# A fused decoder layer with 32 experts: second-layer weights in column halves, the last expert scattered and normed by halves, the last three experts loaded in 2 MB transfers

## The reference

```
logits = rms_norm(x, g_ffn) @ w_router + b_router       # 256 x 32
top_v, top_i = top_k(logits, 4);  gates = softmax(top_v)
for each expert e, for the tokens that chose it:
    u     = xb @ w_e1[e] + b_e1[e]                      # 1024 -> 2048
    x_glu = min(u[..., ::2], 7);  x_lin = clip(u[..., 1::2], -7, 7)
    act   = x_glu * sigmoid(1.702 * x_glu) * (x_lin + 1)
    y     = act @ w_e2[e] + b_e2[e]                     # 1024 -> 1024
x   = x + sum over a token's experts of gate * y
out = rms_norm(x, g_final)
```

## Time and profile before

| what | value |
|---|---|
| median of the runs | 1183.01 us |
| the profiled execution | 1181.18 us |
| its span | 1179.2 us |
| TensorE matmuls busy | 1131.8 us, 96% |
| TensorE weight loads busy | 548.3 us, 47% |
| VectorE busy | 430.9 us, 37% |
| ScalarE busy | 256.7 us, 22% |
| moved by DMA | 447.66 MB, mean 380 GB/s |
| the chain that ended last | TensorE 64%, DMA 30%, VectorE 4%, ScalarE 1% |

### The profile page before, as it was taken

The page is one execution under the profiler, slowest core; times in us unless marked ns, Lnnn a source line. Parts: engine busy times, 40 slices in busy tenths (PEclk is TensorE's granted clock), DMA queues, the critical chain, the costliest instruction groups (busy, mean ns, idle before and its releaser), DMA issues.

```text
span 1179.2 us, 17758 instructions
## 1 busy us (share of the span) xinstructions
PE 1131.8 (96%) x7323; PEld 548.3 (47%) x7323; DVE 430.9 (37%) x836; ACT 256.7 (22%) x441; POOL 21.4 (2%) x22
## 2 busy tenths in 40 slices
PE   7999999999999999999999999999999999999997
PEld 6988999984333333333333333333333333333332
DVE  6889855964222222222222222222222222222223
ACT  5466746332111111111111111111111111111112
POOL 1000200011000000000000000000000000000000
PEclk9999999999999999999999999999999999999999
DMA  7645336789999999999999999999999999999995
GB/s 297 241 147 211 130 140 241 297 336 422 429 426 428 434 430 429 435 430 430 435 431 431 428 437 430 431 428 438 430 429 436 431 430 428 439 428 430 430 425 227
DMA packets 26225, 447.66 MB, mean 380 GB/s; under 512 B 3072, under 2 KB 3456, under 8 KB 5680
## 3 DMA queue, kind: packets, MB, share of 16 engines
q1 hardware_dynamic: 25760, 446.76, 90.0%
q10 hardware_dynamic: 432, 0.42, 0.1%
HBM read 446.12 MB, written 1.05 MB: 379 GB/s over the span
## 4 chain that ended last, share of the span: by engine, by line
PE 64%; DMA 30%; DVE 4%; ACT 1%; issue 1%; DVEq 0%; another core or an unknown queue 0%; SPq 0%; ACTq 0%
PE PS L907 35%; DMA ring<-wexp 29%; PE PS L628 15%; PE PS L900 3%; PE PS L892 3%; PE PS L923 1%; PE PS L677 1%; PE PS L753 1%; DVE ROW L1777 1%; DVE ROW L1780 1%; DVE BRW L1773 1%; PE PS L727 1%; DMA ring<-wblk 1%; DVE ROW L1774 0%; PE PS L990 0%
## 5 line engine op out<-in xcount | busy, mean ns | idle before, releaser
L907 PE MATMUL PS<-ring,MX 128*64 128x512 f32 x1536 | 349.9, 597 | 17.5 <-DMA ring<-wexp 16.3
L907 PEld LDWEIGHTS PS<-ring,MX 128*64 128x64 f32 x1536 | 103.1, 136 | 229.7 <-issue 195.7
L1262 ACT ACTIVATE TAB<-BRW 128x256 f32<-128x256 f32 x64 | 26.7, 417 | 593.6 <-DVE BRW L1773 593.6
L907 PE MATMUL PS<-ring,TAB 128*64 128x512 f32 x512 | 120.0, 600 | 3.5 <-DMA ring<-wexp 3.5
L907 PE MATMUL PS<-EXT,TAB 128*64 128x512 f32 x512 | 119.8, 600 | 3.2 <-DMA EXT<-wexp 3.2
L907 PE MATMUL PS<-EXT,MX 128*64 128x512 f32 x512 | 116.9, 598 | 0.9
L1773 DVE TENSOR_SCALAR BRW<-PS 128x256 f32<-128x256 f32 x64 | 27.2, 425 | 241.1 <-PE PS L907 241.1
L628 PE MATMUL PS<-slot_R 128*128 128x256 f32 (+2 forms) x288 | 90.2, 313 | 0.0
L1315 DVE TENSOR_TENSOR slot_R<-ring,slot_R 128x2048 fp32r<-128x2048 f32 (+1 forms) x37 | 82.6, 2249 | 12.2 <-ACT slot_R L1064 12.1
L1064 ACT ACTIVATE slot_R<-ring 128x2048 fp32r<-128x2048 f32 (+1 forms) x38 | 70.8, 1868 | 38.9 <-DMA ring<-wblk 21.3
L900 PE MATMUL PS<-MX,BRW 64*128 64x512 f32 x264 | 74.2, 640 | 0.8 <-DVE MX L1792 0.8
(11 more groups left out here) (263 smaller groups left out, 1079.2 us busy)
## 6 DMA issues: line engine op xcount, KB each, us to landing
ring<-wexp SPq DMA_DIRECT2D x51, 4096.0 KB, 47.0
EXT<-wexp SPq DMA_DIRECT2D x24, 4096.0 KB, 47.3
ring<-wexp SPq DMA_DIRECT2D x22, 2048.0 KB, 13.4
ring<-wblk SPq DMA_DIRECT2D x36, 1024.0 KB, 4.8
EXT<-wexp SPq DMA_DIRECT2D x13, 2048.0 KB, 13.8
ring<-wexp SPq DMA_DIRECT2D x8, 1024.0 KB, 10.4
EXT<-wexp SPq DMA_DIRECT2D x6, 1024.0 KB, 46.9
BRW<-brow SPq DMA_DIRECT2D x7, 256.0 KB, 5.4
```

Of the source, the lines that this page charges most:

```text
L907: last = mm(PS[g * SLOTS:(g + 1) * SLOTS, b, :], lhsT, rhs[:, g * 512:(g + 1) * 512], start=start, stop=stop)
L1262: fn(SGM[h], GLU, ACT.Sigmoid, scale=ALPHA).then_inc(sgm_ready, 1)
```

## The change

1. The host lays out the second layer's weights by column halves c: chunk 4 now holds, for all eight contraction blocks, columns 0 to 255 of each 512-column half g, and chunk 5 columns 256 to 511. Each matmul is 256 columns wide and there are twice as many.
2. The column halves have a bank each, 6 and 5 (`Y_BANK`). Bank 5 also serves the first layer and the second transposes, so the BE1 bias for bank 5 moves behind `scatter(1)`, and the second-layer bias for bank 5 (`second_bias(1)`) comes after the wait for `at_ready[1]`, in the middle of chunk 4. `gather_scale` moves ahead of it.
3. VectorE copies Y in two halves of 256 columns, and makes the next SELE between the two.
4. In the last expert, column half 0 is scattered (`scatter_part`) in the middle of chunk 5. Squares and products with g_final go by column halves for both token tiles; there is one mean, one root and one reciprocal for both tiles.
5. The last three experts are loaded in 2 MB transfers (before: the last one).

The core of the diff:

```diff
-            for c in range(0, UNROLL * CH - CH, 2):
+            for c in range(0, CH, 2):
                 load_pair(last, last * (UNROLL * CH // 2), c)
-            for c in range(UNROLL * CH - CH, UNROLL * CH):
+            for c in range(CH, UNROLL * CH):
                 load(c, last)
...
-            sp.wait_ge(y_ready, passes * NE)
+            sp.wait_ge(y_ready, passes * (2 * NE))
...
-            def second(w, places):
+            def second(w, c, places):
                 for n in places:
                     f = F_ORDER[n]
                     o = (2 * (f % 4) + f // 4) * SLOTS
-                    last = both_halves(6, AT[:, o:o + SLOTS], w[:, n % 4 * D:(n % 4 + 1) * D], False, n == FT - 1)
+                    for g in range(2):
+                        last = mm(PS[g * SLOTS:(g + 1) * SLOTS, Y_BANK[c], 0:AH], AT[:, o:o + SLOTS],
+                                  w[:, (2 * n + g) * AH:(2 * n + g + 1) * AH], start=False, stop=(n == FT - 1))
+                return last
+            def second_bias(c):
+                for g in range(2):
+                    last = mm(PS[g * SLOTS:(g + 1) * SLOTS, Y_BANK[c], 0:AH], SELE, BE2[:, g, c * AH:(c + 1) * AH],
+                              start=True, stop=False)
+                return last
+            def scatter_part(i, c):
+                for n in range(2):
+                    rows = slice(n * SLOTS, (n + 1) * SLOTS)
+                    last = mm(PS[:, 2 * i + n, c * AH:(c + 1) * AH], SELT[rows, i * P:(i + 1) * P],
+                              Y[rows, c * AH:(c + 1) * AH], start=False, stop=True, skip_group_check=True)
                 return last
...
-                for h in range(2):
-                    both_halves(4 + h, SELE, BE1[:, h * D:(h + 1) * D], True, False)
+                both_halves(4, SELE, BE1[:, 0:D], True, False)
...
-                pe.wait_ge(y_ready, e + 1)
-                for g in range(2):
-                    last = mm(PS[g * SLOTS:(g + 1) * SLOTS, 6, :], SELE, BE2[:, g, :], start=True, stop=False)
-                last.then_inc(chunk_used, 1)
+                pe.wait_ge(y_ready, 2 * e + 2)
+                second_bias(0).then_inc(chunk_used, 1)
                 scatter(0)
                 first_product(chunk(turn, j * CH + 1), 1, early=early).then_inc(chunk_used, 1)
                 scatter(1).then_inc(scattered, 1)
+                both_halves(5, SELE, BE1[:, D:2 * D], True, False)
...
-                last = second(w, range(2))
+                last = second(w, 0, range(4))
                 if not successor:
                     last.then_inc(rsb_full, 1)
                 pe.wait_ge(act_ready, 2 * done + 1)
                 activation_t(1)
-                if halves is not None:
-                    pe.wait_ge(c4_in, halves)
-                second(w, range(2, 4)).then_inc(chunk_used, 1)
                 if successor:
                     pe.wait_ge(selT_a, done + 1)
                     pe.wait_ge(selT_b, done + 1)
                     gather_scale(4)
+                if halves is not None:
+                    pe.wait_ge(c4_in, halves)
+                pe.wait_ge(at_ready[1], done)
+                second_bias(1)
+                second(w, 0, range(4, FT)).then_inc(chunk_used, 1)
                 w = weights(CH1 + 1)
-                pe.wait_ge(at_ready[1], done)
-                last = second(w, range(4, 6))
+                last = second(w, 1, range(4))
                 if not successor:
                     last.then_inc(xg_full, 1)
+                    pe.wait_ge(selT_a, done + 1)
+                    pe.wait_ge(selT_b, done + 1)
+                    pe.wait_ge(y_ready, 2 * done + 1)
+                    for i in range(TT):
+                        last = scatter_part(i, 0)
+                    last.then_inc(moe_done, 1)
                 pe.wait_ge(half_in, 16 * done)
-                second(w, range(6, FT)).then_inc(chunk_used, 1)
+                second(w, 1, range(4, FT)).then_inc(chunk_used, 1)
...
+            pe.wait_ge(y_ready, passes * (2 * NE) + 2)
             for i in range(TT):
-                scatter(i).then_inc(moe_done, 1)
+                pe.wait_ge(ssqf, i + 1)
+                pe.wait_ge(xg_ready, i + 1)
+                scatter_part(i, 1).then_inc(moe_done, 1)
```

More of the change, by code:

```diff
@@ L275, in program @@
         PS = ctx.enter_context(nc.psum_tensor("PS", [P, 8, 512], F32))
+        Y_BANK = [6, 5]
         def bk(b, w=512, p=P):
@@ L1271, in _, with squares @@
             preload(ACT.Sqrt)
[L1272 to L1280, removed]
+            def squares(i, c):
+                act.wait_ge(moe_done, 1 + c * (i + 1))
+                fn(OUTB[:, i, c * BW:(c + 1) * BW].rearrange("p (n w) -> p n w", n=2),
+                   PS[:, 2 * i:2 * i + 2, c * AH:(c + 1) * AH], ACT.Square,
+                   accum_out=S_SQ[:, 2 * i + c:2 * i + c + 1]).then_inc(ssqf, 1)
             def first_half(i):
-                act.wait_ge(rsf, i + 1)
-                act.wait_ge(xg_ready, 2 * i + 1)
+                act.wait_ge(rsf, 1)
+                act.wait_ge(xg_ready, TT + i + 1)
                 fn(OUTB[:, i, 0:BW], XG[:, i, 0:BW], ACT.Copy, scale=S_RS[:, i:i + 1]).then_inc(out_a, 1)
[L1287 to L1292, removed]
+            for c in range(2):
+                for i in range(TT):
+                    squares(i, c)
+            act.wait_ge(varf, 1)
+            fn(S_SD, S_SS, ACT.Sqrt, scale=1.0 / D, bias=col(C_EPS)).then_inc(sdf, 1)
+            for i in range(TT):
+                first_half(i)
             act.wait_ge(out_a, TT)
@@ L1731, in _ @@
             v.tensor_tensor(XT, x_bank, XT, ALU.mult).then_inc(xt_ready, 1)
-            v.memset(Y, 0.0).then_inc(y_ready, 1)
+            for c in range(2):
+                v.memset(Y[:, c * AH:(c + 1) * AH], 0.0).then_inc(y_ready, 1)
             v.memset(RK[:, :, PASSES * NE:PASSES * NE + 1], 1e6)
@@ L1763, in _ @@
                     v.tensor_tensor(SELG, iota2, spread2(RK[:, :, bass.ds(done, 1)]), ALU.is_equal).then_inc(selg_raw, 1)
-                    v.tensor_copy(SELE, hot(bass.ds(T_HOT + (e + 1) % NE, 1))).then_inc(sele_ready, 1)
                     dve.wait_ge(selg_raw, done + 1)
@@ L1790, in _ @@
                     v.tensor_tensor(XT, scale_bank(4), XT, ALU.mult).then_inc(xt_ready, 1)
-                    dve.wait_ge(chunk_used, done * CH + CH)
-                    v.tensor_copy(Y, bk(6)).then_inc(y_ready, 1)
-            dve.wait_ge(gfin_in, 16)
-            for i in range(TT):
[L1796 to L1807, removed]
+                    for c in range(2):
+                        dve.wait_ge(chunk_used, done * CH + CH1 + 1 + c)
+                        v.tensor_copy(Y[:, c * AH:(c + 1) * AH], PS[:, Y_BANK[c], 0:AH]).then_inc(y_ready, 1)
+                        if c == 0:
+                            v.tensor_copy(SELE, hot(bass.ds(T_HOT + (e + 1) % NE, 1))).then_inc(sele_ready, 1)
@@ new lines, in _, with part @@
+            dve.wait_ge(gfin_in, 16)
+            def part(a, c):
+                return a.rearrange("p (n c w) -> p c n w", n=2, c=2)[:, c]
+            for c in range(2):
+                for i in range(TT):
+                    dve.wait_ge(moe_done, 1 + c * (i + 1))
+                    dve.wait_ge(ssqf, 2 * c + i + 1)
+                    v.tensor_tensor(part(XG[:, i, :], c), PS[:, 2 * i:2 * i + 2, c * AH:(c + 1) * AH], part(GF, c),
+                                    ALU.mult).then_inc(xg_ready, 1)
@@ L1808, in _ @@
+            v.tensor_reduce(S_SS, S_SQ.rearrange("p (i n) -> p i n", i=TT), AX_X, ALU.add).then_inc(varf, 1)
+            dve.wait_ge(sdf, 1)
+            v.reciprocal(S_RS, S_SD).then_inc(rsf, 1)
+            dve.wait_ge(rsf, 1)
+            dve.wait_ge(xg_ready, 2 * TT)
+            for i in range(TT):
                 v.tensor_scalar(OUTB[:, i, BW:D], XG[:, i, BW:D], S_RS[:, i:i + 1], None, ALU.mult).then_inc(out_ready, 1)
@@ L1859 @@
     w1 = f["w_e1"][0].reshape(NE, 2, 4, P, 2, 2, AH, 2).transpose(0, 5, 1, 3, 2, 4, 7, 6).reshape(NE, CH1, P, CHW)
-    w2 = f["w_e2"][0].reshape(NE, FT, P, D)[:, F_ORDER].reshape(NE, CH2, 4, P, D).transpose(0, 1, 3, 2, 4).reshape(NE, CH2, P, CHW)
+    w2 = f["w_e2"][0].reshape(NE, FT, P, 2, CH2, AH)[:, F_ORDER].transpose(0, 4, 2, 1, 3, 5).reshape(NE, CH2, P, CHW)
     arrays = {
```

## The result

The changed kernel takes 1229.3 us (median of 4 runs, 1228.74 to 1230.13) against 1183.42 for the kernel before (4 runs): ratio 1.0401, 95% interval 1.0387 to 1.0414. It is 46 us slower. The forecast was 2 us faster, and the range ended at 1183.3.

The account below looks back on a forecast made before the run. HBM traffic was taken to bound the kernel from 729 us on; products ending 1.0 us earlier plus 1.0 us saved after them made 2.0, from a median of 1183.01 to 1181.0 us, range 1178.8 to 1183.3.

Parts of the forecast that it names:

- What bounds the kernel: Whole span: TensorE bounds up to 706.58 us, HBM weight traffic from 729 us on.
- the steady loop: Expert loop on TensorE: column halves add 0.5 us, 27.55 an expert, covered by slack, so they cost nothing.
- The 256-column step: Second-layer products: a 256-column step takes 0.21 us, half the 512-column one, so 16 steps cost the same as 8.
- Rival (1): Steady loop: weight loads show in the shorter steps, 2.7 us an expert, some 60 us slower, 1243; chance 0.06.
- The margin on which it was to decide: Expert loop: TensorE can take 0.75 us more an expert before it decides the time.
- The sentence of the Trainium skill on weight loads: Halved matmuls: a weight load overlaps matmuls in flight only if its row group differs; the prediction's 512-column row spoke against it.
- The last expert: Last expert on TensorE: 2.04 us of new work, yet products end at 1167.6 against 1168.62, 1.0 us earlier.
- E': End of the last expert's products in the changed kernel, forecast at 1167.6 us against 1168.62 before.
- The 2 MB transfers: Loads of chunks 174 to 185: single transfers cost 0.3 us, but chunk 184 lands about 1130.7 in place of 1135.3.
- The tail: After the last products: last issue at +6.05 us against +7.7, end at +9.55 against +10.55, 1.0 us saved.
- The sum: Whole kernel: 1.0 us from products ending earlier plus 1.0 from the work after them, 2.0 us saved.

Follow-up runs that it names:

- e10: The changed kernel, TensorE loop of 4 experts moved by 149 skipped instructions ahead of it, plus e5's earlier signal: 1180.81 us, ratio 0.9989.
- e5: e1 with the signal releasing VectorE's leftover XT scaling in the last expert moved to the first half of chunk 4: 1178.83 us, ratio 0.9972.
- e3: The kernel before with 135 never-executed matmuls (271 instructions) at the end of TensorE's loop body: 1181.61 us, ratio 1.0007.
- e1: The changed kernel with TensorE's expert loop covering 2 experts per iteration in place of 4: 1181.95 us, ratio 1.0003.
- e4: The changed kernel with its loop of 4 experts and 149 never-executed instructions ahead of the loop: 1183.54 us, ratio 1.0015.
- e7: The kernel before with skipped instructions only, 201 ahead of TensorE's loop and 267 at its body's end: 1232.58 us, ratio 1.0429.
- e8: e7 with 349 skipped instructions ahead of the loop, so that it stands where e4's does: 1181.39 us, ratio 0.9995.
- e6: e5 without the 2 MB transfers, experts 29 and 30 again in 4 MB pairs: 1180.83 us, ratio 0.9995.

## Why the prediction was wrong, point by point

- **What bounds the kernel**: right for the kernel before. In the changed one TensorE bounds it to the end.
- **The step that failed** is the one that sums up the steady loop: "Sum: 0.5 us, 27.55 an expert. Is it covered? [...] So 0.5 costs nothing, and TensorE meets the DMA near 880 us in place of 729". What is executed was priced, and too high: 27.14 us an expert, 0.09 more than before. (So TensorE meets the DMA far earlier than 880 where the stops are gone: the chain passes to weight loads at 740.6 in e10 and at 796.5 in e5.) What was left out is the code: 64 more instructions in each of four experts, and a loop that starts 201 instructions later, make it touch 8 blocks of instructions where it touched 6 (7 without the unseen instructions of e3), and that costs 11 us for each of six jumps (e1, e4, e7, e8). Nothing of it is in the trace of before but the x counts and the 25 instruction transfers, for a loop that fits shows no price.
- **The 256-column step**: right. 48 instructions (24 steps) take 5.18 us in the chain, 0.216 each, with the load hidden.
- **Rival (1)** forecast 1243 us, TensorE the bound throughout, and gave that 0.06. The outcome looks like it, but its cause, loads that show, is refuted by the line above. The margin on which it was to decide, 0.75 us an expert, was the useful part: 66 us less 24 of margin, and 3.5 at the end, is 45.5; counted from the first product of expert 0 the products end 47.1 later (938.2 against 891.1).
- **The sentence of the Trainium skill on weight loads** (page "TensorE: Matmul & The Clock Gate", section "The mechanism" of Part 3), by which a load overlaps only when its row group differs, doesn't hold at 256 columns either, by the same step. The same section also lets a load be pulled ahead when it goes to a background weight buffer; whether the hidden loads here did so, no run shows.
- **The last expert**: the wait for ScalarE's copy was 0.56 (forecast 0.48), the scatter 1.06 (1.06), E' in e5 1168.1 (1167.6). Wrong was the sentence "the early scatter's input is ready 0.5 us after chunk 4": it counted the copy and not what stands before it in VectorE's queue. That cost 1.9 us and, through the clock, 1.5 more (e5).
- **The 2 MB transfers**: the 0.3 us of slower pace are too small to be told; in e5 chunk 187 lands at 1145.7 (1145.4 forecast) and the last half at 1131.0 + 34.6 = 1165.6 (1165.1), within the spread of runs. With the halves they are worth 2.7 us (e5 against e6), the halves without them next to nothing (e6 against before).
- **The tail**: in the changed kernel the last issue comes 6.1 us after the products (1224.27 less 1218.14; forecast 6.05) and the end of the span 9.8 (9.55). In e5 it is 9.9, against 10.55 before: 0.65 saved.
- **The sum**, 2.0 us, is borne out in its mechanism. e10, the change with nothing else but the stops and the late signal mended, saves 1.3 us (0.2 to 2.4). In its profile chunk 187 lands 22.4 us before the products end, where it was 23.5 before, 1.1 gained (1.0 forecast), and the tail gains 0.65 (1.0 forecast). e5's 3.3 (2.2 to 4.4) is more than the sum, by the earlier loads of the smaller loop (865.9 against 867.6), which nothing in the prediction foresaw. The edit as given had the gain buried under 3 us at the end and 47 in the loop.

## What to carry to other kernels

When an edit adds instructions inside a hardware loop, count the loop's instructions on that engine and the blocks of 256 that they touch, before pricing what they do; the instruction queue's packets in the profile tell whether code is fetched again, and "issue" idle at the first instruction of a loop's body is its mark. Code that is never executed counts too, since it moves the loop. Where an operation is moved ahead, walk its engine's queue and ask for each operation before it what that one waits for, leftovers of a loop's last iteration above all. A gain of a few tenths of a per cent at the end of a kernel is only seen when both are clean, and two profiles are compared from a common event rather than from the start of the span: here the first product of the expert part stood anywhere from 277.4 to 280.0 us.

## What the runs showed of the hardware

- TensorE's code stays on the chip across a jump back when the loop touches 7 blocks of 256 instructions and is reloaded when it touches 8 (by my count, with the 35 to 60 instructions that e3 asks for): 28 transfers against 81 or 82. A jump back then costs two stops, 2.7 to 3.9 and 4.6 to 5.5 us in the changed kernel, and some 2.5 us lost to half the clock. In a loop that stays it costs 0.09 us (e1, e4). I took the weight stream (431 GB/s beside it) for a reason of the long second stop, but ran nothing that tells.
- Skipped instructions cost nothing but their room: e8 has 616 of them and stands at 0.9995.
- After a wait of 1.9 us for one copy the granted clock fell to 0.50 for about 3 us. The fall came when the work had already resumed (from 1167.0 in e1, where it resumed at 1165.56), and without the wait it didn't come (e5).
- Whatever else differed, the loads ran some 1.5 us earlier by the end of the kernel beside TensorE's loop over two experts than beside the one over four (chunk 187 after 865.4 to 866.6 us against 867.2 to 868.0). The cause is open.
